# Router logits made tile by tile, three experts ranked and read first, latent weights read behind the last store

## The chip, the cores and the metric

The kernel is one program on one core of a Trainium2 chip. Its engines are TensorE (PE in the profile), VectorE (DVE), ScalarE (ACT), GpSimd (POOL) and SyncE (SP), which here only issues transfers; 16 DMA engines move data between the chip's memory (HBM) and the on-chip SBUF. Each engine works through its own list of instructions in order and waits on semaphores for the others. The metric is the device time of one execution in microseconds.

## The reference, cut to what matters

1024 tokens of width 1024 pass through a first block (windowed attention, a gated recurrence and a delta-rule recurrence, side by side). Its output, with 16 meta tokens ahead of it (L = 1040 rows), passes through two layers. Each layer ends in a mixture of experts:

```python
p_g = softmax(xf @ wr_g + br_g)            # 4 groups, the best one is taken
logit_e = xf @ wr_e + br_e                 # 32 experts, 8 in a group
top_v, top_i = top_k(sel, 2)               # two experts in the chosen group
y = (silu(xb @ w_gate[e]) * (xb @ w_up[e])) @ w_down[e]
out[token] += y * gate
```

Layer 0 mixes by pooled windows ahead of its experts. After its experts the shared latent is computed: `c = rmsnorm(h) @ w_dkv`, then keys and values by `w_uk` and `w_uv`, and queries by `w_dq` and `w_uq`. Layer 1 mixes by attention over that latent, then an output projection, then its experts; the end is an RMS norm. All is float32.

## The kernel before

Rows are held as tiles of 128: eight of them (NT = 8), and in layer 0 a ninth, first in order, for the 16 meta rows (NS = 9). One python function per engine and stage writes that engine's list; `pe_moe`, `act_moe`, `dve_moe`, `pool_moe` and `sp_moe` (from L2933) put a layer together: routing turns, the table, the experts, overflow blocks.

**Routing turns.** `turns(n, depth)` interleaves the steps of the tiles: in turn t each step d works on tile t - d, the latest step first. In layer 0 the steps are row scaling for the pool (d = 0), pooled windows (d = 1), the group map and the sum into h (d = 2: VectorE L1805, GpSimd L1834, ScalarE's square sum L1538), root and scaled rows (d = 3: L1612, L1609, L1926), transposes of the rows (d = 4: TensorE L1878, ScalarE copies L1907), logits (d = 5: TensorE in `mm`, L218). In layer 1 they are the output projection (d = 0: 32 records of TensorE a tile), root and rows, transposes and logits. `mm` and `transpose` write float32; one product in the code is two records in the trace. Before the change `routed` says at which tiles logits are made: the meta tile alone, tiles 0 to 3 at tile 3, tiles 4 to 6 at tile 6, tile 7 alone. The weights `wr` (128x36) are the stationary side and give logits transposed, 36 rows high; ScalarE copies them out (L1913), TensorE transposes them back (L1895), VectorE adds the bias (L1933). PSUM banks are given out in the order of the list that `plan_layer` builds; `rb.free(key)` is the wait for the bank's last user.

**Table.** VectorE alone, save for two TensorE steps: it picks experts, counts tokens per expert, sorts the 32 experts by count (`y.key` = count times 32 plus `y.backward`, L2011; eight ranks at a time, each counted by the semaphore `sorted`) and computes which token goes to which row of which block. TensorE turns that into the list `idx` by one-hot products (16 or 18 of 128x128 by 41 columns).

**Experts.** 25 blocks of 128 rows. The 18 experts with most tokens (N_BIG) have a block each, the other 14 share seven blocks in pairs of 64 rows (`PAIR_AT` says at which places). An expert with more tokens than its rows needs an overflow block, worked serially behind the 25 (`sp_over` and its like), as many as the data ask for. `sp_experts` loads weights in order of rank through four buffers, 2 MB of gate and up (L2121) and 1 MB of down (L2126) for each; `weights_of` waits for the sort and reads the expert's number from `by_count`. Loads 0 to 2 go out at the start, load 3 when gathers 0 and 1 have landed, later ones when TensorE has used the buffer. GpSimd gathers each block's rows from `xn_dram` (L2264) once `idx` is there; TensorE transposes them (L2139), multiplies gate and up, transposes the hidden rows (L2161), multiplies down; SyncE stores each block's result (L2279).

**Latent stage.** In the last blocks of layer 0 `sp_latent_ahead` also loads `wc`, the rope table, `w_uv`, `w_uq` (behind block 22) and `w_uk` (behind block 23). When the last stores have landed, GpSimd gathers the two expert rows of each token (L2378), VectorE sums them into h (L2372), ScalarE squares and takes the root (L1538, L1612), VectorE scales the rows (L2612), TensorE transposes (L2527) and multiplies. `dve_latent` first scales `w_uq` (three instructions, L2592) and `w_uv` (two, L2594); `w_uk` is scaled ahead of the fourth tile's sum.

Of the kernel before, what the change touches and what calls it, by code (L numbers as in the profile page):

```python
# [57 lines left out]
LOADED = [(_rank, _i) for _i in range(NM) for _rank in RANKS[_i]]  # L58
SLOTS = NBLK * P
# [127 lines left out]
def build(nc, io):  # L187
    ctx = ExitStack()
    with ctx:
# [27 lines left out]
        def mm(e, out, lhsT, rhs, start, stop):  # L217
            return e.matmul(out, lhsT, rhs, start=start, stop=stop, skip_group_check=True)  # L218
# [1398 lines left out]
        def routed(y, p):  # L1617

            s = y.slots[p]
            if s == NT:  # L1620
                return NT, NT
            return {3: (0, 3), NT - 2: (4, NT - 2), NT - 1: (NT - 1, NT - 1)}.get(s)

        layers, ring_before, table_before = [], [o1], [bk_]

        def plan_layer(layer):
# [17 lines left out]
            y.ci, y.full = take(P), take(NE)  # L1644
# [6 lines left out]
            for d, p in turns(y.ns, y.depth):  # L1651
# [6 lines left out]
                if d == y.norm_at + 2 and routed(y, p):  # L1658
                    order += [(("lgT", p), "S"), (("lg", p), "V")]
# [189 lines left out]
        def dve_ids(e, y):  # L1849
# [8 lines left out]
            e.tensor_scalar(y.backward, y.io32, -1.0, float(NE), ALU.mult, ALU.add).then_inc(*y.ids.up())  # L1858
# [11 lines left out]
        def pe_route(e, y, d, p):  # L1870
# [9 lines left out]
            elif d == y.norm_at + 2 and routed(y, p):  # L1880
                s0, s1 = routed(y, p)
                n = s1 + 1 - s0
                cols = slice(P * s0, P * (s1 + 1))
                key = ("lgT", p)
# [3 lines left out]
                for k in range(KD):  # L1888
                    m = mm(e, y.rb.bank[key][0:NR, 0:P * n], y.wr[:, k, :], y.xgT[:, k, cols], k == 0, k == KD - 1)
                m.then_inc(*y.rb.fill(key))  # L1890
                e.wait_ge(*y.rb.empty(key))
                key = ("lg", p)
                wait_all(e, y.rb.free(key))
                for j in range(n):
                    m = e.transpose(y.rb.bank[key][:, NR * j:NR * j + NR], y.lgT[0:NR, P * (s0 + j):P * (s0 + j + 1)], ident[0:NR, 0:NR])  # L1895
                m.then_inc(*y.rb.fill(key))

        def act_route(e, y, d, p):
# [10 lines left out]
            elif d == y.norm_at + 2 and routed(y, p):  # L1909
                s0, s1 = routed(y, p)  # L1910
                key = ("lgT", p)
                e.wait_ge(*y.rb.full(key))
                e.activation(y.lgT[0:NR, P * s0:P * (s1 + 1)], y.rb.bank[key][0:NR, 0:P * (s1 + 1 - s0)], ACT.Copy,  # L1913
                             bias=0.0).then_inc(*y.rb.drain(key, "S"))

        def dve_route(e, y, d, p):
# [11 lines left out]
            elif d == y.norm_at + 2 and routed(y, p):  # L1928
# [1233 lines left out]
```

## Time and profile before

| | us |
|---|---|
| median of 3 runs | 2188.95 |
| lowest, highest | 2187.75, 2190.74 |
| the profiled execution | 2186.3 |
| its span | 2184.6 |

In the profiled execution TensorE is busy for 1960.5 us (90%), VectorE for 807.5, ScalarE for 533.0, GpSimd for 188.3. By stage, in microseconds from the start of the span: the first block to about 679; routing turns of layer 0 to 787; table to 825; experts to 1131; latent stage from there and attention to 1649; routing turns of layer 1 to 1793; table to 1828; experts to 2136; the last sums and norm to the end. Times in rows are from the start of the span. A timeline row is start, duration, engine, line, operation, output from input, the shape of one instruction and how many were merged; the bracket is the idle time before and what ended it.

### The profile page before, as it was taken

The numbers are of one execution on the slowest core, as the hardware profiler recorded it, in microseconds if no ns is written. First come the engines' busy times: TensorE is split into PE (matmuls) and PEld (weight loads), VectorE is DVE, ScalarE is ACT, GpSimd is POOL, SyncE is SP. The second block draws the span as 40 slices with busy tenths as digits, with TensorE's granted clock in tenths as the row PEclk, the third lists the DMA queues.
The fourth block names the chain that finished last, engine by engine and source line by source line (L and its number), as shares of the span: only waits on it lengthen the run. The fifth ranks groups of instructions, "written<-read, shape, count | busy, mean of one in ns | idle before, by whom it ended". The sixth has DMA issues, their size and how long they took to land. (4 is left out here: it accounts for less than half of the span.)

```text
span 2184.6 us, 27881 instructions
## 1 busy us (share of the span) xinstructions
PE 1960.5 (90%) x10832; PEld 1121.7 (51%) x10832; DVE 807.5 (37%) x1849; ACT 533.0 (24%) x1295; POOL 188.3 (9%) x283
## 2 busy tenths in 40 slices
PE   8999999889997948999967999999999975999990
PEld 4545554578444824444424657677674433444440
DVE  1115557767254452111114534444451124111115
ACT  1003334433011311111123433333331110111112
POOL 0000002001262201000002000000000000000003
PEclk9999999899998968999988999999999986999995
DMA  3500100020011128999983000000010007999986
GB/s 135 224 32 1 39 20 4 1 80 4 34 65 44 57 115 342 410 424 424 426 361 122 22 1 1 1 1 1 1 78 23 39 29 314 364 426 423 425 356 261
DMA packets 51389, 334.67 MB, mean 153 GB/s; under 512 B 6832, under 2 KB 7152, under 8 KB 33200
## 3 DMA queue, kind: packets, MB, share of 16 engines
q1 hardware_dynamic: 39376, 289.63, 32.6%
q0 software_dynamic: 11872, 43.13, 5.3%
q8 instruction: 92, 1.51, 0.3%
q14 instruction: 49, 0.40, 0.1%
HBM read 285.48 MB, written 47.25 MB: 152 GB/s over the span
## 5 line engine op out<-in xcount | busy, mean ns | idle before, releaser
L218 PE MATMUL psum<-arena 64*64 64x64 f32 (+9 forms) x9424 | 1813.4, 385 | 120.5 <-DVE arena L2070 26.8
L218 PEld LDWEIGHTS psum<-arena 128*128 128x128 f32 (+3 forms) x9424 | 966.7, 165 | 908.2 <-issue 794.6
L2178 DVE TENSOR_TENSOR arena<-psum,arena 128x256 f32<-128x256 f32 x50 | 21.2, 425 | 430.4 <-ACT arena L2228 421.5
L1538 ACT ACTIVATE arena<-arena 128x1024 f32<-128x1024 f32 x43 | 45.4, 1056 | 249.9 <-DVE arena L2921 101.6
L2264 POOL DMA_INDIRECT arena<-xn_rows,arena x50 | 47.1, 943 | 685.6 <-PE psum L2139 453.7
L2228 ACT ACTIVATE arena<-psum 128x256 f32<-128x256 f32 x50 | 19.2, 385 | 328.2 <-PE psum L218 328.2
L2834 ACT ACTIVATE arena<-psum,arena 128x1024 f32<-128x1024 f32 (+8 forms) x72 | 50.2, 699 | 188.6 <-DVE arena L2870 188.6
L1239 ACT ACTIVATE arena<-psum 128x256 f32<-128x256 f32 (+3 forms) x128 | 43.9, 356 | 101.4 <-PE psum L218 90.3
L2139 PE MATMUL psum<-arena 128*128 128x128 f32 x400 | 53.7, 279 | 15.6 <-DMA arena<-xn_rows,arena 15.6
L2221 ACT ACTIVATE arena<-psum 128x512 f32<-128x512 f32 x50 | 29.9, 597 | 148.0 <-PE psum L218 148.0
L2863 DVE TENSOR_TENSOR psum<-psum,arena 128x128 f32<-128x128 f32 (+2 forms) x72 | 20.4, 283 | 103.5 <-PE psum L218 103.2
L2139 PEld LDWEIGHTS psum<-arena 128*128 128x128 f32 x400 | 46.6, 144 | 16.9 <-DMA arena<-xn_rows,arena 15.9
L2251 DVE COPY arena<-psum 128x512 f32<-128x512 f32 x50 | 34.6, 692 | 53.5 <-PE psum L218 53.5
L2209 ACT ACTIVATE arena<-psum 128x512 f32<-128x512 f32 x50 | 29.9, 598 | 98.8 <-PE psum L2139 98.8
L2372 DVE SCALAR_TENSOR_TENSOR arena<-arena 128x1024 f32<-128x1024 f32 (+1 forms) x34 | 43.6, 1281 | 25.5 <-DMA arena<-expert_rows,arena 24.0
L2865 DVE TENSOR_REDUCE arena<-psum 128x1 f32<-128x1024 f32 (+8 forms) x72 | 50.8, 706 | 2.5
L2378 POOL DMA_INDIRECT arena<-expert_rows,arena x34 | 34.6, 1019 | 192.6 <-issue 135.9
L2886 DVE COPY arena<-psum 128x512 f32<-128x512 f32 (+3 forms) x48 | 22.8, 490 | 76.0 <-PE psum L2789 75.9
L2789 PE MATMUL psum<-arena 128*128 128x128 f32 x352 | 48.9, 273 | 0.0
L381 ACT ACTIVATE arena<-psum 128x512 f32<-128x512 f32 (+1 forms) x26 | 15.5, 597 | 127.3 <-PE psum L218 127.3
L395 DVE TENSOR_TENSOR arena<-psum,arena 128x512 f32<-128x512 f32 x16 | 10.9, 689 | 84.2 <-ACT arena L376 84.0
L639 DVE TENSOR_TENSOR arena<-psum,arena 128x512 f32<-128x512 f32 (+1 forms) x32 | 18.8, 651 | 62.4 <-PE psum L218 62.4
(303 smaller groups left out, 1298.1 us busy)
## 6 DMA issues: line engine op xcount, KB each, us to landing
arena<-in_w_exp SPq DMA_DIRECT2D x64, 2048.0 KB, 18.7
arena<-in_w_exp SPq DMA_DIRECT2D x64, 1024.0 KB, 20.6
expert_rows<-arena SPq DMA_DIRECT2D x66, 512.0 KB, 15.8
arena<-in_x SPq DMA_DIRECT2D x16, 512.0 KB, 4.3
xn_rows<-arena SPq DMA_DIRECT2D x16, 512.0 KB, 2.6
arena<-in_w_out SPq DMA_DIRECT2D x8, 512.0 KB, 7.8
arena<-in_w_o SPq DMA_DIRECT2D x1, 4096.0 KB, 12.1
out<-arena SPq DMA_DIRECT2D x8, 512.0 KB, 4.2
```

Source lines behind the costliest of these rows:

```text
L218: return e.matmul(out, lhsT, rhs, start=start, stop=stop, skip_group_check=True)
L1239: e.activation(dst, src, ACT.Copy, bias=0.0).then_inc(*ring.drain((i, name), "S"))
L1538: return e.activation(junk, h[:, s, :], ACT.Square, accum_out=sq_sum[:, s:s + 1])
L2139: m = e.transpose(four(ring.bank[key])[:, k, :], xe[:, P * (4 * hf + k):P * (4 * hf + k + 1)], ident)
L2209: e.activation(y.xt[b % 2][:, 4:8, :], four(y.ex.bank[key]), ACT.Copy, bias=0.0).then_inc(*y.ex.drain(key, "S"))
L2251: e.tensor_copy(y.y[b % 3][:, half_cols(0)], y.ex.bank[key]).then_inc(*y.ex.drain(key, "V"))
L2264: e.indirect_dma_start(out=xe, out_offset=None, in_=xn_dram[:, :], in_offset=bass.IndirectOffsetOnAxis(idx.bitcast(I32)[:, block:block + 1 ...
L2372: e.scalar_tensor_tensor(out=h[0:n, s, :], in0=c[j][0:n, :], scalar=gates[0:n, s, j:j + 1], in1=h[0:n, s, :], op0=ALU.mult, op1=ALU.add).t ...
L2378: e.indirect_dma_start(out=c[j][0:n, :], out_offset=None, in_=y_dram[:, :], in_offset=bass.IndirectOffsetOnAxis(dest.bitcast(I32)[0:n, s, ...
L2789: m = e.transpose(four(sd.bank[key])[:, j, :], pb[:, kp:kp + P], ident)
L2834: e.activation(pb[0:n, p0:p1], part_bank(key).bank[key][0:n, 0:p1 - p0], ACT.Exp, bias=mx[0:n, 0:1], scale=SCALE, accum_out=rsu[0:n, u:u + ...
L2865: e.tensor_reduce(mx[0:n, u:u + 1], bk[0:n, 0:p1 - p0], AX.X, ALU.max).then_inc(*V.up())
```

## The change

- Logits are made for each tile by itself: the tile's rows are the stationary side (128x128), `wr` moves (36 columns), and the result comes out with tokens on partitions. The copy by ScalarE, the small transposes and the function `routed` go.
- Experts 0, 1 and 2 get ranks 0, 1 and 2 whatever their counts: `y.backward` is raised by 65536 times 3, 2 and 1 for them, by two more VectorE instructions. `weights_of` returns their fixed addresses without a wait, so loads 0 to 2 go out when the routing turns are over.
- `w_uq`, `w_uv` and `w_uk` are loaded behind the last expert's store; VectorE's scaling of `w_uq` and `w_uv` moves ahead of the third tile's sum.
- ScalarE takes one root of a constant behind the overflow blocks of each layer, which loads the root's table there.

```diff
@@ -1614,13 +1617,6 @@
-        def routed(y, p):
-
-            s = y.slots[p]
-            if s == NT:
-                return NT, NT
-            return {3: (0, 3), NT - 2: (4, NT - 2), NT - 1: (NT - 1, NT - 1)}.get(s)
@@ -1655,8 +1651,8 @@
-                if d == y.norm_at + 2 and routed(y, p):
-                    order += [(("lgT", p), "S"), (("lg", p), "V")]
+                if d == y.norm_at + 2:
+                    order.append((("lg", p), "V"))
@@ -1855,7 +1851,11 @@
-            e.tensor_scalar(y.backward, y.io32, -1.0, float(NE), ALU.mult, ALU.add).then_inc(*y.ids.up())
+            e.tensor_scalar(y.backward, y.io32, -1.0, float(NE), ALU.mult, ALU.add).then_inc(*V.up())
+
+            e.tensor_scalar(y.lead, y.io32, float(N_FIRST), 0.0, ALU.subtract, ALU.min).then_inc(*V.up())
+            e.wait_ge(*V.last())
+            e.scalar_tensor_tensor(out=y.backward, in0=y.lead, scalar=-float(LEAD), in1=y.backward, op0=ALU.mult, op1=ALU.add).then_inc(*y.ids.up())
@@ -1877,22 +1877,13 @@
-            elif d == y.norm_at + 2 and routed(y, p):
-                s0, s1 = routed(y, p)
-                n = s1 + 1 - s0
-                cols = slice(P * s0, P * (s1 + 1))
-                key = ("lgT", p)
+            elif d == y.norm_at + 2:
+                key = ("lg", p)
                 e.wait_ge(*y.m_router)
                 e.wait_ge(*y.rb.empty(("xt", p, 1)))
                 wait_all(e, y.rb.free(key))
                 for k in range(KD):
-                    m = mm(e, y.rb.bank[key][0:NR, 0:P * n], y.wr[:, k, :], y.xgT[:, k, cols], k == 0, k == KD - 1)
-                m.then_inc(*y.rb.fill(key))
-                e.wait_ge(*y.rb.empty(key))
-                key = ("lg", p)
-                wait_all(e, y.rb.free(key))
-                for j in range(n):
-                    m = e.transpose(y.rb.bank[key][:, NR * j:NR * j + NR], y.lgT[0:NR, P * (s0 + j):P * (s0 + j + 1)], ident[0:NR, 0:NR])
+                    m = mm(e, y.rb.bank[key][:, 0:NR], y.xgT[:, k, P * s:P * (s + 1)], y.wr[:, k, :], k == 0, k == KD - 1)
                 m.then_inc(*y.rb.fill(key))
...
@@ -2111,6 +2093,8 @@
             rank = LOADED[n][0]
+            if rank < N_FIRST:
+                return io["w_exp"][y.n * NE + rank]
             e.wait_ge(*y.sorted.at(rank // 8 + 1))
@@ -2395,14 +2379,13 @@
-                assert top_uq <= base_b2 + 2 * WG and {n % 4 for later in range(b + 1, NM) for n in y.of[later]} == {2, 3}
-                e.wait_ge(*y.ex.full(("gu", b)))
-                e.dma_start(w_uv, io["w_uv"]).then_inc(d_lu.sem, 16)
-                e.dma_start(w_uq, io["w_uq"]).then_inc(d_lu.sem, 16)
-            if b == NM - 2:
-                assert top_uq + 2 * MH * NOPE <= base_b2 + 3 * WG and {n % 4 for n in y.of[NM - 1]} == {3}
-                e.wait_ge(*y.ex.full(("gu", b)))
-                e.dma_start(w_uk, io["w_uk"]).then_inc(d_uk.sem, 16)
+
+        def sp_latent_behind(e):
+
+            assert top_uq + 2 * MH * NOPE <= base_b2 + 3 * WG
+            e.dma_start(w_uq, io["w_uq"]).then_inc(d_lu.sem, 16)
+            e.dma_start(w_uv, io["w_uv"]).then_inc(d_lu.sem, 16)
+            e.dma_start(w_uk, io["w_uk"]).then_inc(d_uk.sem, 16)
@@ -2434,6 +2417,8 @@
             sp_store(e, y, NM - 1)
+            if y.n == 0:
+                sp_latent_behind(e)
@@ -2587,12 +2572,13 @@
         def dve_latent(e):
-            e.wait_ge(*m_lu)
-            for k in range(3):
-                e.tensor_scalar(w_uq[:, k, :], w_uq[:, k, :], col("q_norm", k), None, ALU.mult).then_inc(*(lat_w if k == 2 else V).up())
-            for k in range(2):
-                e.tensor_scalar(w_uv[:, k, :], w_uv[:, k, :], col("kv_lat", k), None, ALU.mult).then_inc(*lat_w.up())
             for d, s in turns(NS, LAT):
+                if (d, s) == (0, 2):
+                    e.wait_ge(*m_lu)
+                    for k in range(3):
+                        e.tensor_scalar(w_uq[:, k, :], w_uq[:, k, :], col("q_norm", k), None, ALU.mult).then_inc(*(lat_w if k == 2 else V).up())
+                    for k in range(2):
+                        e.tensor_scalar(w_uv[:, k, :], w_uv[:, k, :], col("kv_lat", k), None, ALU.mult).then_inc(*lat_w.up())
@@ -2954,6 +2940,8 @@
             act_experts(e, y)
             act_over(e, y)
 
+            e.activation(scr[:, 0:1], one_col, ACT.Sqrt).then_inc(*S.up())
```

The bias is then added per tile (`y.lg[:, s, :]` from the bank's 36 columns and `y.br`), and ScalarE's branch for logits is removed. `N_FIRST` is 3 and `LEAD` is 65536.

## Rows read from the trace of the kernel before

**Rows 1.** The page: memory traffic in GB/s, 40 equal slices of the span.

```profile
GB/s 135 224 32 1 39 20 4 1 80 4 34 65 44 57 115 342 410 424 424 426 361 122 22 1 1 1 1 1 1 78 23 39 29 314 364 426 423 425 356 261
```

**Rows 2.** Timeline of layer 0's routing turns, TensorE and VectorE.

```profile
734.12 7.17 PE L218 MATMUL psum<-arena 128*128 128x256 f32 x48 [0.34 <-issue]
...
742.56 14.16 PE L218 MATMUL psum<-arena 128*128 128x256 f32 x64 [0.34 <-issue]
...
757.76 1.09 PE L1878 MATMUL psum<-arena 128*128 128x128 f32 x8
...
775.07 7.02 PE L218 MATMUL psum<-arena 128*36 128x384 f32 x16 [3.45 <-issue]
...
775.38 1.28 DVE L1926 SCALAR_TENSOR_TENSOR arena<-arena 128x1024 f32<-128x1024 f32 x1
...
782.96 1.09 PE L1878 MATMUL psum<-arena 128*128 128x128 f32 x8
...
787.39 0.20 DVE L1933 TENSOR_TENSOR arena<-psum,arena 128x36 f32<-128x36 f32 x1 [4.06 <-PE psum L1895]
```

**Rows 3.** Timeline of layer 1's routing turns, TensorE and VectorE.

```profile
1735.41 20.89 PE L218 MATMUL psum<-arena 128*128 128x512 f32 x48
...
1758.27 13.90 PE L218 MATMUL psum<-arena 128*128 128x512 f32 x32
...
1776.81 1.97 PE L1878 MATMUL psum<-arena 128*128 128x128 f32 x8 [3.76 <-DVE arena L1926]
...
1779.51 8.29 PE L218 MATMUL psum<-arena 128*36 128x384 f32 x16 [0.73 <-issue]
...
1793.11 0.20 DVE L1933 TENSOR_TENSOR arena<-psum,arena 128x36 f32<-128x36 f32 x1 [4.05 <-PE psum L1895]
```

**Rows 4.** Timeline of the first weight load, gather and transposes, layers 0 and 1.

```profile
805.34 0.36 SPq L2121 DMA_DIRECT2D arena<-in_w_exp  x1
...
825.26 1.18 POOL L2264 DMA_INDIRECT arena<-xn_rows,arena  x1 [52.45 <-DVE arena L2088]
...
831.57 1.97 PE L2139 MATMUL psum<-arena 128*128 128x128 f32 x8 [6.84 <-DMA arena<-xn_rows,arena]
...
1828.43 0.98 POOL L2264 DMA_INDIRECT arena<-xn_rows,arena  x1 [178.23 <-DVE arena L2088]
...
1836.66 1.97 PE L2139 MATMUL psum<-arena 128*128 128x128 f32 x8 [8.74 <-DMA arena<-xn_rows,arena]
```

**Rows 5.** Timeline from the last stores of layer 0 into the latent stage.

```profile
1125.99 5.01 SPq L2279 DMA_DIRECT2D expert_rows<-arena  x2
...
1133.57 2.88 DVE L2592 TENSOR_SCALAR arena<-arena 128x1536 f32<-128x1536 f32 x3 [4.58 <-DMA arena<-in_w_uq]
...
1142.31 0.94 POOL L2378 DMA_INDIRECT arena<-expert_rows,arena  x1 [66.59 <-issue]
...
1146.83 1.28 DVE L2372 SCALAR_TENSOR_TENSOR arena<-arena 128x1024 f32<-128x1024 f32 x1 [9.06 <-DMA arena<-expert_rows,arena]
...
1151.51 1.28 ACT L1612 ACT_TABLE_LOAD   x1
...
1171.51 0.69 DVE L2618 COPY arena<-psum 128x512 f32<-128x512 f32 x1 [9.30 <-PE psum L2527]
```

**Rows 6.** Timeline of layer 0's table, the one-hot products.

```profile
816.83 7.90 PE L218 MATMUL psum<-arena 128*128 128x41 f32 x36 [13.64 <-DVE arena L2070]
```

**Rows 7.** Busy time and granted clock, 1770 to 1790 us; clock after the engines.

```profile
1770.00:1790.00 20.00, 14.71 (x49) 6.67 (x47) 3.86 (x6) 4.79 (x11) 0.00 (x0) 0.74 0.13 53
```

**Rows 8.** Chain of waits, layer 1's last store and first gather: start, us, what.

```profile
2136.05 4.50 DMA expert_rows<-arena
...
2142.05 0.94 POOL arena L2378
```

**Rows 9.** Timeline of the last stage, first sum.

```profile
2146.46 1.29 DVE L2372 SCALAR_TENSOR_TENSOR arena<-arena 128x1024 f32<-128x1024 f32 x1 [12.11 <-DMA arena<-expert_rows,arena]
```

**Rows 10.** The page, costliest groups: the gathers of expert rows.

```profile
L2264 POOL DMA_INDIRECT arena<-xn_rows,arena x50 | 47.1, 943 | 685.6 <-PE psum L2139 453.7
```

## What the change will do to the time

> **What bounds the kernel now.** The page's 40 slices of 54.6 us come first [rows 1]: memory traffic stands at 340 to 426 GB/s only in the expert streams, layer 0's in slices 16 to 21 and layer 1's in 35 to 39; elsewhere it is low and cannot be the bound. The change touches five places around these streams, so the timeline of each was read: the routing turns of both layers [rows 2, 3], the table and the first rows of the experts [rows 4], and the passage from the last expert of layer 0 to the latent stage [rows 5]. The reader should look for what released the first TensorE instruction of each stage. It is a chain, not a queue of work: logits, then table, then a gather, then TensorE; last store, then a gather, then sum, root, transpose, TensorE. Whatever leaves those chains comes off the end in full, because what follows is ordered behind them. Inside the streams TensorE runs back to back and nothing of the change lies there.
>
> **Logits, layer 0.** Today the first tile's logits are made alone, tiles 0 to 3 in one batch of 16 records of 512 columns, tiles 4 to 6 in one of 384, and tile 7 alone; each batch is followed by a ScalarE copy and small transposes. The new form has 16 records per tile with 128x128 weights and 36 columns. No row shows 36. Nearest are 128x128 weights with 41 columns: 7.90 us for 36, 0.22 us each, at the low clock [rows 6]. At the high clock, the ordinary turn has 48 records in 7.17 us [rows 2]; 16 of them have 256 columns (0.22 us each, as the batch's 0.43 us for 512 tells), which leaves 0.11 us each for the 32 narrow ones. So a tile costs 1.8 us high and 3.5 us low; I take 1.8 in the turns, which have no pause, and lean to 3.5 at the tail, where TensorE pauses. In a turn it waits 0.34 us [rows 2], so 1.8 us adds 1.45 to each of five turns, +7.3 us. Removed there: 14.16 - 7.17 = 7.0 us of the batch, 1.0 us of copy and transposes behind it (742.56 + 14.16 to 757.76) and 0.8 us of the same for the first tile. Net -1.5. The end is where it pays: from 775.07 to 782.96 the last tile's transposes stand behind the batch of three, 7.9 us, though their rows are ready at 776.7. With one tile in the batch's place this is 1.8 to 3.5 us. From 782.96 to the last logits at 787.39 is 4.4 us; afterwards it is transposes 1.1 to 2.0, copy 0.7, logits 1.8 to 3.5, 3.7 to 6.3 in all. The last logits come 8.1 us earlier at the high clock, 3.9 at the low. I take **-5.5**.
>
> **Logits, layer 1.** The turns hold 32 records of 512 columns and are all TensorE [rows 3]: four tiles add 7.2 us and the batch takes away 20.89 less 13.9, 7.0 us, and 1.0 us behind it: -0.8. The tail: before, transposes at 1776.81, the batch of three in 8.29 us from 1779.51, last logits at 1793.11. Afterwards two of the three are made while TensorE waits for tile 6's rows anyway (it waits 3.76 us there), and the third lies between transposes. Following the same chain (ScalarE copy 1.1, root 0.3, reciprocal 0.2, row scaling 1.3, transposes 1.1, copy 0.7, logits) gives 1784.1 at the high clock and 1788.4 at the low. The granted clock there is 0.74 of full speed [rows 7], a mix of the two levels, and the same transposes take 1.97 us there and 1.09 in layer 0 [rows 2]. I take **-6.0**, between -4.7 and -9.0.
>
> **Experts 0 to 2 read early.** Their three loads go out at 805.34 behind the sort; now they go behind the last logits, some 18 us sooner. This does not start the stream sooner by 18 us: TensorE starts when the first gather lands, and that is issued after the table (825.26). The gain is only that the gather runs on idle DMA engines. It takes 6.3 us in layer 0 and 8.2 in layer 1 while the loads run [rows 4]; the first gather of the last stage, with nothing beside it, takes 4.4 [rows 8, 9]. So **-1.8** and **-3.7** (bounds 1.0 to 2.3 and 2.5 to 4.3). The loads of later experts wait for buffers that TensorE frees and so shift with it. What hides the early loads is the table, 38 us from the last logits to the gather against 22 us for 9.4 MB at 424 GB/s [rows 1]. Behind these issues on SyncE stand only the fourth expert's loads, which wait for gathers 0 and 1 anyway. The forced ranks add two short VectorE operations with a wait ahead of layer 0's first rows: **+0.3**; in layer 1 they lie in an idle stretch.
>
> **Latent weights behind the last store.** They stand in the queue ahead of the last stores today. The last store goes out at 1131.0 (the second of the pair in [rows 5]) and the first gather of the sums starts at 1142.31, 11.3 us later. In layer 1, with nothing beside it, the store lands 4.50 us after 2136.05 and the gather starts at 2142.05, 6.0 us [rows 8]. Without the 4.4 MB the gather should start near 1137. But the same 4.4 MB, 10.3 us of all engines, now run from 1133 to about 1144, under the gathers. A gather that is issued with about this much still to come took 8.2 us (layer 1, [rows 4]), not the 4.5 us seen here [rows 5]: it lands at 1145.3 to 1146.7 where it landed at 1146.8. The weights are then through, so the second should follow more closely. I take 1.7 us for both, between 0 and 3.7. The DMA page of the Trainium skill, "DMA: Bandwidth & Descriptors", section "Queues, rings and completion order", has each engine take turns between queues a packet at a time. By an equal share a gather would lose only its own 1.2 us of transfer, and this part would be worth some 2 us more; the trace of gathers beside weight loads says 3.8 us lost, and I go by that.
>
> The scaling of these weights on VectorE (2.88 us for three rows, so about 4.2 for all five) today hides in its wait for the store. It moves ahead of the third sum, where VectorE next waits 9.30 us for TensorE [rows 5]; 4.2 of that is free. Should the weights land after 1160 this cover is gone, and 1 us late costs 1 us. The gathers of later tiles wait for that sum, but have 12 us.
>
> **Root's table.** Its load of 1.28 us stands between square sum and root [rows 5], and behind it wait row scaling, the second tile's sum and, through ScalarE, the copy that lets TensorE start on the latent products: -1.3, with the gather part's 1.7 **-3.0** (bounds 0 and -5). In the last stage the load ends before VectorE is done with the second sum: nothing. The Trainium skill ("ScalarE: Activation LUTs", "What ACT_TABLE_LOAD costs") adds 1.38 us of draining to a load; no row here shows it, the root starts 20 ns after the load. With it the sum would be 1.4 us better.
>
> **Sum.** -5.5 - 6.0 - 1.8 - 3.7 + 0.3 - 3.0 = **-19.7 us**. The profiled execution took 2186.3 us (span 2184.6 and 1.7 around it), which gives 2166.6; the median of the runs is 2.65 above it, so 2188.95 - 19.7 = **2169.2**. All best ends give -28.5 (2160.5), all worst -11.6 (2177.4).
>
> **Rivals.** *The streams take the starts back.* DMA is full in them, and if loads, not TensorE, set their end, an earlier first gather changes nothing, and with the sums' gathers equally late only the logits and root's table are left: -11.5 - 1.3 + 0.3 = -12.5, 2176.5. For: 424 GB/s throughout, within 2 of the highest of the page [rows 1]. Against: TensorE has no pause in 200 us of them, and the loads are released by it. *The narrow records are dear*: 0.22 us in the turns too, because 128 columns of weights are loaded for 36 moved. Nine turns at +1.7 are +15.3, at the low ends of both tails: -3.9 - 4.7 + 15.3 - 5.2 - 3.0 = -1.5, 2187.5. Against: the 32 narrow ones of layer 0's turns. *Slower, by an overflow block*: ranking three fixed experts first pushes others out of the 18 full blocks of 128 rows; one of those with more than 64 tokens needs a serial block behind all others. Its price, from rows: weights about 10 us, gate and up 7, evictions and transposes 2.5, down 3.7, store and its landing 5, issue 2, about 30 us. A single one decides: 2169.2 + 30 = 2199. Against: 50 gathers, none extra, before [rows 10], and the reference's own router on its inputs gives 14 and 12 experts above 64 tokens, so with experts 0 to 2 added 15 and 15 places are needed of 18. It also needs other inputs. *The change doesn't do what it says*: if the loads still waited for the sort (they don't in the diff), the 5.5 us are missing: 2174.7, inside the range.
>
> **Chances.** The sum 0.72, streams take back 0.13, dear records 0.08, overflow 0.03, something worse that I don't see 0.04. The range of the sum, widened to the first rival and towards the second: **2160 to 2182**. What a measurement here can tell from no change is about 0.2%, 4.4 us. Faster 0.87, same 0.08, slower 0.05.
>
> **What would show it.** The last logits of layer 0 near 782 and the first weight loads at once behind them; first gather to TensorE 4.5 us in both layers; narrow groups of 16 in 1.8 us in the turns. First gather of the sums 6 us behind the last store but 8 us to land; no table load between square sum and root; VectorE's five scalings inside its wait for TensorE. Wrong if a turn of layer 0 is much above 9.9 us, if the last of the stream does not shift with its first, or if VectorE waits for the latent weights.

## The result and the profile after

| | us |
|---|---|
| before, median of 4 runs (lowest to highest) | 2189.84 (2187.75 to 2192.07) |
| after, median of 4 runs (lowest to highest) | 2171.03 (2164.63 to 2174.86) |
| ratio after to before, 95% interval | 0.9919 (0.9897 to 0.9940) |
| the profiled execution of after, its span | 2170.03, 2168.3 |

The change makes the kernel 18.8 us faster (2189.84 - 2171.03); the interval of the ratio is 13 to 23 us. The forecast was 19.7 us less, 2169.2.

The page of after has the traffic where [rows 1] had it, but for slices 15 (204 for 115) and 33 (81 for 29), into which the early loads of layers 0 and 1 now fall ahead of the streams, and 16 and 34, which have less (245 for 342, 278 for 314); and it has the same 50 gathers of expert rows as [rows 10], so no overflow block:

```profile
GB/s 136 213 34 11 39 20 4 1 81 4 2 98 44 49 204 245 404 423 425 424 368 158 23 1 1 1 1 1 1 78 23 29 81 278 379 426 423 425 354 263
...
L2248 POOL DMA_INDIRECT arena<-xn_rows,arena x50 | 47.3, 945 | 672.4 <-PE psum L2123 447.9
```

The timeline of TensorE in the routing turns of layer 0, after, answers [rows 2]. An ordinary turn first, then the tail:

```profile
728.89 1.07 PE L1878 MATMUL psum<-arena 128*128 128x128 f32 x8
729.80 8.90 PE L221 MATMUL psum<-arena 128*128 128x256 f32 x64
738.53 1.07 PE L1878 MATMUL psum<-arena 128*128 128x128 f32 x8
```

```profile
773.52 1.07 PE L1878 MATMUL psum<-arena 128*128 128x128 f32 x8
776.34 3.60 PE L221 MATMUL psum<-arena 128*128 128x36 f32 x16 [1.75 <-issue]
779.74 1.95 PE L1878 MATMUL psum<-arena 128*128 128x128 f32 x8
782.42 3.60 PE L221 MATMUL psum<-arena 128*128 128x36 f32 x16 [0.73 <-issue]
```

A turn takes 9.64 us (728.89 to 738.53), and its 64 records 8.90 where 48 took 7.17: 1.73 us for the 16 narrow ones, 0.11 us each. In the tail the same 16 take 3.60 us. The last of them releases VectorE, and SyncE's first weight load follows at once (timeline of both, after):

```profile
786.06 0.19 DVE L1916 TENSOR_TENSOR arena<-psum,arena 128x36 f32<-128x36 f32 x1 [5.89 <-PE psum L221]
...
786.32 0.33 SPq L2105 DMA_DIRECT2D arena<-in_w_exp  x1
```

The tail of layer 1 (TensorE, after) answers [rows 3]; its last logits are added at 1781.55:

```profile
1767.43 1.95 PE L221 MATMUL psum<-arena 128*128 128x36 f32 x16 [0.78 <-issue]
1769.21 1.88 PE L1878 MATMUL psum<-arena 128*128 128x128 f32 x8
1771.82 3.60 PE L221 MATMUL psum<-arena 128*128 128x36 f32 x16 [0.73 <-issue]
1775.23 1.95 PE L1878 MATMUL psum<-arena 128*128 128x128 f32 x8
1777.91 3.60 PE L221 MATMUL psum<-arena 128*128 128x36 f32 x16 [0.73 <-issue]
```

First gather and first transposes of both layers, after, answer [rows 4]. From the gather to TensorE it is 4.65 us in layer 0 and 4.31 in layer 1 (before 6.31 and 8.23):

```profile
823.89 1.18 POOL L2248 DMA_INDIRECT arena<-xn_rows,arena  x1 [49.81 <-DVE arena L2070]
...
828.54 1.97 PE L2123 MATMUL psum<-arena 128*128 128x128 f32 x8 [5.18 <-DMA arena<-xn_rows,arena]
...
1816.86 0.98 POOL L2248 DMA_INDIRECT arena<-xn_rows,arena  x1 [173.49 <-DVE arena L2070]
...
1821.17 1.97 PE L2123 MATMUL psum<-arena 128*128 128x128 f32 x8 [4.83 <-DMA arena<-xn_rows,arena]
```

The passage into the latent stage, after, answers [rows 5]:

```profile
1127.69 0.32 SPq L2263 DMA_DIRECT2D expert_rows<-arena  x1
...
1128.06 0.43 SPq L2386 DMA_DIRECT2D arena<-in_w_uq  x1
...
1133.72 0.94 POOL L2362 DMA_INDIRECT arena<-expert_rows,arena  x1 [60.79 <-issue]
...
1135.28 1.28 ACT L2943 ACT_TABLE_LOAD   x1
...
1142.28 1.28 DVE L2356 SCALAR_TENSOR_TENSOR arena<-arena 128x1024 f32<-128x1024 f32 x1 [16.29 <-DMA arena<-expert_rows,arena]
1145.99 1.28 DVE L2356 SCALAR_TENSOR_TENSOR arena<-arena 128x1024 f32<-128x1024 f32 x1 [2.42 <-DMA arena<-expert_rows,arena]
...
1155.24 2.86 DVE L2579 TENSOR_SCALAR arena<-arena 128x1536 f32<-128x1536 f32 x3
...
1166.37 0.69 DVE L2604 COPY arena<-psum 128x512 f32<-128x512 f32 x1 [4.37 <-PE psum L2512]
```

The first and the second sum are the additions of the first tile's two expert rows; each waits for a gather of its own. The gather starts 5.71 us behind the end of the last store's issue, where it was 11.31 (1131.00 to 1142.31). But the first sum comes 8.56 us behind it instead of 4.52, and the second 3.71 behind the first. Before, that was 2.20, as the timeline of before shows:

```profile
1146.83 1.28 DVE L2372 SCALAR_TENSOR_TENSOR arena<-arena 128x1024 f32<-128x1024 f32 x1 [9.06 <-DMA arena<-expert_rows,arena]
1149.03 1.28 DVE L2372 SCALAR_TENSOR_TENSOR arena<-arena 128x1024 f32<-128x1024 f32 x1 [0.91 <-DMA arena<-expert_rows,arena]
```

The intervals below are read from the timelines of one profiled execution each; "route start" is GpSimd's first instruction of the routing turns, "to last logits" ends where VectorE adds the bias to them, "to last store" runs from the experts' first transposes to the start of the last store's issue, "last store to first gather" from the end of that issue, "c0" is the first latent product, "c2" the third tile's transposes in the latent stage. The c0 to c2 of busy all is left out, because unused products stand ahead of c0 there.

| interval, us | before | before again | after | after again | logits only | early only | latent only | latent late | busy tail | busy all | best |
|---|---|---|---|---|---|---|---|---|---|---|---|
| start to route start, layer 0 | 679.3 | 682.0 | 681.9 | 686.5 | 678.9 | 681.0 | 684.0 | 679.7 | 686.8 | 683.3 | 684.8 |
| to last logits, layer 0 | 108.1 | 107.8 | 104.1 | 104.1 | 100.9 | 108.8 | 107.6 | 104.2 | 100.0 | 100.4 | 99.5 |
| first gather to TensorE, layer 0 | 6.3 | 6.2 | 4.7 | 5.0 | 6.3 | 5.3 | 6.5 | 4.8 | 4.6 | 4.8 | 5.7 |
| to last store, layer 0 | 299.1 | 299.9 | 299.2 | 299.9 | 298.7 | 299.1 | 299.6 | 300.4 | 300.1 | 296.9 | 295.8 |
| last store to first gather of the sums | 11.3 | 10.2 | 5.7 | 5.1 | 11.1 | 10.1 | 4.5 | 6.1 | 6.1 | 5.5 | 5.7 |
| first gather of the sums to first sum | 4.5 | 4.5 | 8.6 | 8.7 | 4.5 | 4.3 | 9.1 | 4.2 | 8.7 | 8.5 | 4.1 |
| first sum to second | 2.2 | 1.7 | 3.7 | 3.5 | 2.1 | 2.0 | 3.8 | 2.2 | 2.6 | 3.1 | 2.5 |
| second sum to transposes | 5.1 | 5.1 | 3.8 | 3.8 | 5.1 | 5.1 | 5.1 | 3.8 | 3.8 | 3.8 | 3.8 |
| c0 to c2 | 26.6 | 23.6 | 24.1 | 23.9 | 26.7 | 23.5 | 26.5 | 26.2 | 23.7 | | 26.4 |
| route start to last logits, layer 1 | 143.8 | 142.3 | 139.1 | 139.3 | 139.8 | 142.2 | 143.8 | 140.1 | 134.2 | 134.2 | 134.2 |
| first gather to TensorE, layer 1 | 8.2 | 8.4 | 4.3 | 4.9 | 7.4 | 4.4 | 8.4 | 5.1 | 4.9 | 5.0 | 5.0 |
| to last store, layer 1 | 299.4 | 300.2 | 298.8 | 300.0 | 300.1 | 298.6 | 299.0 | 298.5 | 299.7 | 295.3 | 295.2 |

### The profile page after: what moved, and what is told of

It reads as the page before. It is cut to its first block and busy times, and to the rows that moved or that the text cites. A ratio compares the mean times of both kernels' runs of the same rounds, so it can differ in the third digit from the quotient of the medians.

```text
span 2168.3 us, 28117 instructions
## 1 busy us (share of the span) xinstructions
PE 1961.4 (90%) x10975; PEld 1146.7 (53%) x10975; DVE 809.5 (37%) x1863; ACT 531.4 (25%) x1290; POOL 189.3 (9%) x283
## 5 line engine op out<-in xcount | busy, mean ns | idle before, releaser
L221 PE MATMUL psum<-arena 128*128 128x512 f32 (+12 forms) x9584 | 1817.1, 384 | 117.5 <-DVE arena L2052 26.7
L221 PEld LDWEIGHTS psum<-arena 128*128 128x128 f32 (+3 forms) x9584 | 994.5, 169 | 887.3 <-issue 774.8
L2907 DVE TENSOR_TENSOR arena<-arena,psum 128x512 f32<-128x512 f32 x16 | 11.0, 688 | 84.3 <-PE psum L221 84.3
```

## The experiments

The theory is that of the sum: logits, early loads and latent stage each take their term off a chain. The rivals are that the streams take the earlier starts back, that narrow records are dear, and, once the result was seen, that the clock takes a part of the logits' gain. The first three kernels carry one part of the change each; the early root was not run alone.

| kernel | median us (runs) | before beside it | ratio, 95% |
|---|---|---|---|
| logits only | 2174.94 (2172.70 to 2179.48) | 2189.58 | 0.9942 (0.9922 to 0.9961) |
| early only | 2178.38 (2175.48 to 2182.95) | 2189.58 | 0.9957 (0.9939 to 0.9974) |
| latent only | 2190.40 (2185.95 to 2194.56) | 2189.58 | 1.0008 (0.9995 to 1.0021) |
| after again | 2173.92 (2168.73 to 2175.22) | 2189.58 | 0.9922 (0.9902 to 0.9943) |
| latent weights behind the gathers | 2170.65 (2170.30 to 2180.51) | 2190.64 | 0.9910 (0.9884 to 0.9935) |
| busy tail | 2164.16 (2161.22 to 2166.91) | 2190.64 | 0.9876 (0.9850 to 0.9903) |
| busy all | 2158.68 (2149.51 to 2164.35) | 2190.64 | 0.9854 (0.9813 to 0.9894) |
| latent late | 2164.88 (2163.48 to 2166.06) | 2189.75 | 0.9890 (0.9872 to 0.9908) |
| best | 2153.15 (2152.22 to 2153.57) | 2189.75 | 0.9838 (0.9824 to 0.9853) |

### Logits tile by tile, alone

The kernel before with only this part (`mm` in the new form, the copy, the small transposes and `routed` gone):

```diff
-                    m = mm(e, y.rb.bank[key][0:NR, 0:P * n], y.wr[:, k, :], y.xgT[:, k, cols], k == 0, k == KD - 1)
...
+                    m = mm(e, y.rb.bank[key][:, 0:NR], y.xgT[:, k, P * s:P * (s + 1)], y.wr[:, k, :], k == 0, k == KD - 1)
```

> The kernel before with the logits tile by tile and nothing else. My theory, corrected by the trace of the changed kernel: the two tails each gain, but at the low level of TensorE's clock, 3.6 us for 16 narrow records, so last logits come about 4 us earlier in layer 0 (from the start of its routing turns) and 4.7 in layer 1, and the median falls by 8 to 9 us. A turn of layer 0 takes 9.6 us instead of 8.4, paid back by the missing batch. Rival, that the profiled gain is an accident of the clock: the two intervals from the start of the routing turns to the last logits change by less than 2 us each and the median by under 4.

Measured: 14.6 us faster than before (2189.58 - 2174.94; 8.5 to 17.1 by the interval), where 8 to 9 was expected. Layer 1 gives 4.0 in the profile, layer 0 gives 7.2, 11.2 together; the rest of the 14.6 isn't explained. That dear narrow records cost the gain is ruled out: they cost 0.11 us in the turns. Why layer 0 gives more than in after (4.0) stands in the tail of this kernel's timeline (TensorE): the first narrow group there still takes 1.95 us, and only what follows is slow.

```profile
768.95 1.07 PE L1871 MATMUL psum<-arena 128*128 128x128 f32 x8
771.76 1.95 PE L218 MATMUL psum<-arena 128*128 128x36 f32 x16 [1.74 <-issue]
773.54 1.90 PE L1871 MATMUL psum<-arena 128*128 128x128 f32 x8
776.18 3.60 PE L218 MATMUL psum<-arena 128*128 128x36 f32 x16 [0.73 <-issue]
```

That is 1.7 us of the 3.2, and 0.3 is the forced ranks, which this kernel lacks; the rest lies in the first turns, which also run in part at the lower level (clock 0.84 over their first 40 us, 0.81 in after). The same code gains more or less by where in it the clock falls.

### Experts 0 to 2 read early, alone

```diff
+            if rank < N_FIRST:
+                return io["w_exp"][y.n * NE + rank]
```

with the raised `y.backward`.

> The kernel before with experts 0 to 2 ranked first and read early, nothing else. My theory: only the first gather's flight shortens, from 6.3 to about 4.6 us in layer 0 and from 8.2 to about 4.3 in layer 1, minus 5.6 us in all, kept to the end of both streams; two VectorE operations cost 0.3 us. Median lower by 5 us. Rival, that the stream is bound by its transfers and takes the start back: the interval from the first rows on TensorE to the last store grows by as much as the flight shrinks, and the median moves by under 1 us. A second rival, that the stream starts 19 us sooner and gains far more: median lower by over 10 us.

Measured: 11.2 us faster (5.7 to 13.4 by the interval). In the profile the gathers' flights are 1.0 and 3.8 us shorter, and the experts take 299.1 and 298.6 us, no longer than in before: the streams don't take the start back. The profile's intervals give 4.8 us of gathers and 0.8 of the second stream, 5.6 in all, the low edge of the interval. Intervals that no line of this part touches give more: c0 to c2 3.2, layer 1's turns 1.6, last store to first gather of the sums 1.2. All three are as short in a second execution of before, so they are not shown to be the change's. The second rival on record has the right size, over 10 us, but not the mechanism: the first gather still starts 37.9 us behind layer 0's last logits, so the stream starts no 19 us sooner. So the forecast of 5.2 holds for the mechanism; a part of the 11.2 of the median isn't explained.

### Latent weights behind the last store, alone

```diff
+            e.dma_start(w_uq, io["w_uq"]).then_inc(d_lu.sem, 16)
+            e.dma_start(w_uv, io["w_uv"]).then_inc(d_lu.sem, 16)
+            e.dma_start(w_uk, io["w_uk"]).then_inc(d_uk.sem, 16)
```

behind `sp_store(e, y, NM - 1)`, the scaling ahead of the third sum, and no early root.

> The kernel before with the latent weights behind the last store (and their scaling moved), nothing else, root's table still loaded late. My theory: the first gather of the sums starts 6 us earlier after the last store, but lands 8.5 us after its start where it took 4.5, and the second 3.7 us behind the first, so the second sum starts about 0.4 us earlier than before and TensorE's first latent transposes as well; median lower by 0 to 1 us. Rival, that the earlier start carries through: 3 us or more at TensorE's transposes.

Measured: 0.8 us slower over ten runs, between 1.1 faster and 4.6 slower. Its timeline of VectorE and GpSimd has the two sums 9.13 and 12.91 us behind the gather, where before has 4.52 and 6.72:

```profile
1140.40 0.94 POOL L2378 DMA_INDIRECT arena<-expert_rows,arena  x1 [60.52 <-issue]
...
1149.53 1.28 DVE L2372 SCALAR_TENSOR_TENSOR arena<-arena 128x1024 f32<-128x1024 f32 x1 [15.62 <-DMA arena<-expert_rows,arena]
1153.31 1.28 DVE L2372 SCALAR_TENSOR_TENSOR arena<-arena 128x1024 f32<-128x1024 f32 x1 [2.49 <-DMA arena<-expert_rows,arena]
```

What the earlier gather gains, the 4.4 MB beside it take back in full.

### After and before once more

Both without an edit, to see how much an interval of a profile moves by itself.

> The changed kernel once more, to see what differs from one execution to the next. If the 2.7 us that it was late ahead of the routing turns, where the code is the same, and the 2.5 us that it gained between the second and third latent product are the clock's, then another profile shows either one changed while the intervals of the changed steps agree within 0.5 us. If they belong to the change, both stand again.

> The kernel before once more, one look. If the start of the routing turns and the step from the first to the third latent product move with the clock from execution to execution, this profile differs from the first of before by microseconds there, while the gather's flights (6.3 and 8.2 us), store to gather (11.6) and gather to first sum (4.5) stand within 0.5 us. If they are constants of the kernel, all agree within 0.5 us.

Measured: after again 2173.92, ratio 0.9922, where the first time gave 0.9919; one execution of before took 2184.49. In the table most steps of the change repeat within 0.6 us. The exceptions are layer 1's turns of before, 143.8 and 142.3, so their gain is between 2.9 and 4.7; last store to first gather of the sums, 11.3 and 10.2 in before, so that gain is between 4.5 and 6.2; and the streams, which move by up to 1.2. Two intervals that no edit touches move more: start to route start is between 678.9 and 687.2 us in twelve profiles with the same code up to there, and c0 to c2 is 26.6 or 23.6 in two profiles of before. The windows of the two profiles of before show what it is in c0 to c2 (before, then before again; stretch, its length, busy time of PE, PEld, DVE, ACT and POOL, granted clock, DMA share, GB/s): the same stretch has a clock of 0.82 and 0.90.

```profile
1157.00:1187.00 30.00, 26.40 (x86) 16.72 (x86) 11.59 (x23) 9.14 (x25) 5.61 (x6) 0.82 0.33 105
```

```profile
1157.00:1187.00 30.00, 24.52 (x91) 15.96 (x90) 13.26 (x25) 10.40 (x28) 5.70 (x6) 0.90 0.33 110
```

So the end of a single profile tells a gain only to some us, and an interval around a step to one or two.

### Latent weights behind the gathers

From after: the call of `sp_latent_behind` leaves `sp_experts` and stands behind the overflow blocks, with a wait for the second pair of gathers.

```diff
-            if y.n == 0:
-                sp_latent_behind(e)
...
+            if y.n == 0:
+                wait_all(e, m_cl[1])
+                sp_latent_behind(e)
```

> The changed kernel with the latent weights read only when the gathers of the first two tiles have landed. My theory, that the weights slow these gathers: first sum 4.5 us after the first gather instead of 8.6, second sum 2.1 behind it instead of 3.6, so TensorE's first latent transposes come 5.5 us earlier than in the changed kernel, and the weights, landing some 22 us after the first gather, still meet VectorE in its wait for TensorE; median 4 to 5.5 us below the changed kernel. Rival, that gathers are slow there for another reason (their own queue, the store just before): first sum stays 8.6 us after the gather, and the median rises by up to 5 us because the weights come late. A second rival: the gathers are fast but VectorE waits for the weights ahead of the third sum and gives it back.

Measured: 2170.65, which can't be told from after. The profile is of its slowest execution, 2180.5, where the other four took 2170.3 to 2173.9. The sums come 4.35 and 6.45 us behind the gather again, so it was the 4.4 MB that delayed them. But now VectorE waits for the weights (its timeline in this kernel; the loads go out from 1152.15):

```profile
1157.31 0.89 DVE L2596 TENSOR_SCALAR arena<-arena 128x1024 f32<-128x1024 f32 x1
1165.92 2.88 DVE L2577 TENSOR_SCALAR arena<-arena 128x1536 f32<-128x1536 f32 x3 [7.73 <-DMA arena<-in_w_uv]
1168.72 1.41 DVE L2579 TENSOR_SCALAR arena<-arena 128x1024 f32<-128x1024 f32 x2
1170.04 2.67 DVE L2356 SCALAR_TENSOR_TENSOR arena<-arena 128x1024 f32<-128x1024 f32 x2
```

c0 to c2 takes 31.2 us in it, 7.1 more than in after. Of this 6.0 is TensorE's wait ahead of the second tile's products (7.91 us for 1.93), the rest its clock. So the wait that is taken away at the gather comes back at the scaling, in front of the third tile's sums: the second rival on record.

### Latent late: the scaling moved as well

The same kernel, with the scalings two tiles later:

```diff
-                if (d, s) == (0, 2):
+                if (d, s) == (0, 4):
...
-                if (d, s) == (0, 3):
+                if (d, s) == (0, 5):
```

> The changed kernel with the latent weights read when the first two tiles' gathers have landed, and their scaling moved two tiles later, ahead of the fifth and sixth tiles' sums, where VectorE waits for TensorE anyway. My theory, from the run before: first sum 4.4 us after the gather, second 2.1 behind, no wait of VectorE for the weights, so the steps from first gather to the third tile's latent transposes take about 38.5 us where the changed kernel took 44.3 and the run with the early scaling 45; median 5 us below the changed kernel, about 2166. Rival, that the delay is only moved on: the fifth tile's sum comes late, TensorE waits there, and from the third tile's transposes to the start of layer 1's routing turns it takes over 3 us more than the 464.2 of all other runs.

Measured: 2164.88; the ratio is 0.9890 against 0.9919 and 0.9922 of after, some 6.6 us, though the intervals overlap (0.9872 to 0.9908, 0.9897 to 0.9940). In its timeline of VectorE both sums are early, and no wait for the weights is left:

```profile
1137.52 1.28 DVE L2356 SCALAR_TENSOR_TENSOR arena<-arena 128x1024 f32<-128x1024 f32 x1 [12.27 <-DMA arena<-expert_rows,arena]
1139.75 1.29 DVE L2356 SCALAR_TENSOR_TENSOR arena<-arena 128x1024 f32<-128x1024 f32 x1 [0.95 <-DMA arena<-expert_rows,arena]
...
1154.72 1.28 DVE L2356 SCALAR_TENSOR_TENSOR arena<-arena 128x1024 f32<-128x1024 f32 x1 [4.45 <-DMA arena<-expert_rows,arena]
1160.48 0.69 DVE L2602 COPY arena<-psum 128x512 f32<-128x512 f32 x1 [4.48 <-PE psum L2510]
```

From the first gather to c0 this wins 5.9 us. The later gathers now run beside the weights (the wait at 1154.72 is for one of them), but TensorE waits no longer for it: 1.93 us ahead of the second tile's products, as in before and after. From c0 to layer 1's route start it takes 490.2 us instead of 488.4; all of this is in c0 to c2 (26.2 for 24.1), which differs by 3 us between the two profiles of before, and from c2 on it is 464.0 for 464.2. So nothing shows that any of the 5.9 is given back.

### Busy tail: the clock held up

From after: TensorE multiplies the identity with ones, 512 columns wide, into the bank that the logits are to fill, while it waits for ScalarE's copy. The products are used by nobody.

```diff
+        def keep_busy(e, bank, n):
+            for _ in range(n):
+                mm(e, four(bank), ident, bc_mid(ones, 4), True, True)
...
-                e.wait_ge(*y.rb.empty(("xt", p, 1)))
                 wait_all(e, y.rb.free(key))
+                if p >= y.ns - 3:
+                    keep_busy(e, y.rb.bank[key], 2 if y.n == 0 and p == y.ns - 2 else 1)
+                e.wait_ge(*y.rb.empty(("xt", p, 1)))
```

> The changed kernel with one or two wide products of constants, 512 columns, ahead of the logits of the last three tiles of either layer, in TensorE's pauses; results unused. My theory, that the narrow records cost 3.6 instead of 1.9 us at the tails because the clock is at its low level there: with the pauses filled the clock holds, the last logits come 3 us earlier in each layer and the median falls by up to 6 us. Rival, that 0.22 us is the narrow record's own price after a pause or that the clock falls anyway: the last logits come 1 to 4 us later by the added work.

Measured: 2164.16. The windows of the last turns of layer 0, columns as above (the clock is the third from the end), in before, after and busy tail:

```profile
774.00:790.00 16.00, 10.57 (x44) 5.01 (x44) 4.21 (x33) 4.27 (x8) 0.00 (x0) 0.86 0.08 33
```

```profile
774.00:790.00 16.00, 9.54 (x46) 8.82 (x44) 5.05 (x39) 5.01 (x9) 0.08 (x1) 0.56 0.25 86
```

```profile
774.00:790.00 16.00, 12.76 (x83) 10.24 (x81) 7.07 (x39) 4.90 (x9) 2.49 (x2) 1.00 0.29 101
```

After loses the high level in the tail (0.56, where 0.50 is the level of 1.2 GHz), which before mostly has (0.86). With the pauses filled it is 1.00, and last logits come 100.0 and 134.2 us behind route start, 4.1 and 4.9 less than in after. That shows that the clock, not the order of work, was what kept the gain small.

### Busy all: the same at the other pauses

The same products also in the table (12 behind the last logits, 12 ahead of the one-hot products), ahead of the first gather's transposes (5) and ahead of the latent stage (20, and 3 ahead of its first product).

> As the one before, with such products also in TensorE's waits of the table (12 and 12), of the first gather (5) and of the latent stage's first rows (20 and 3). My theory: the clock stays at its high level over these waits; the first expert block's products take 6.9 us instead of 9 to 10 in both layers, the first latent products fall from 11.6 to about 8 us for the first tile and likewise the second; with the tails 12 to 16 us below the changed kernel. Rival, that the clock falls all the same: the products run at the low level, last twice as long, and push the table's products and first rows back, 5 to 20 us slower than the changed kernel.

Measured: 2158.68. The experts take 296.9 and 295.3 us instead of 299.2 and 298.8, as the stream now begins at the high level (clock 1.00 over the first 20 us in both layers, 0.78 and 0.85 in after), and from last logits to first gather it is 36.6 and 34.1 us instead of 37.8 and 35.3. The latent stage gained nothing, against the expectation: the unused products end 3.60 us ahead of the first transposes, these still take 1.97 us, and from the first gather of the sums to c2 it takes 45.5 us (44.5 in after).

### Best: both together

Latent late and busy all, with 18 products instead of 20 and without the 3.

> The one before together with the unused wide products in TensorE's pauses: at the tails of the routing turns, in the table's waits, ahead of the first expert rows, and 18 ahead of the first latent rows, none between these and the latent products. My theory: the two savings add, since one shortens a chain and the other the work at its end: about 2152 to 2155, with the first expert block at the high level of the clock in both layers and the first latent products at 8 to 9 us instead of 11.6. Rival, that the clock's low stretches only move to other places: the low stretches of the profile sum to as much as in the changed kernel, 244 us, and the median is that of the run with the tails filled, 2164, or above.

Measured: 2153.15, 1.6% below before (0.9824 to 0.9853 of it) and 17.9 below the first median of after. The mean granted clock over the span is 0.970 (before 0.948, after 0.944). The rival, that the low stretches only move, falls. The timeline of TensorE at the first expert of layer 0, after and best: the first 16 products take 10.17 and 7.11 us.

```profile
831.29 10.17 PE L221 MATMUL psum<-arena 128*128 128x512 f32 x16 [0.78 <-ACT arena L2193]
```

```profile
828.98 7.11 PE L221 MATMUL psum<-arena 128*128 128x512 f32 x16 [0.78 <-ACT arena L2204]
```

In layer 0's table the unused products of best run into the landing of the first gather: the transposes follow them without a pause, 5.7 us behind the gather, where busy all has a pause of 0.63 and 4.8 us.

And the passage to the latent stage in best (TensorE), with the products of the same tile in latent late below it: the unused products end 0.51 us ahead of the transposes, so they delay nothing, and the transposes take 1.09 us where after has 1.97.

```profile
1139.45 1.09 PE L2524 MATMUL psum<-arena 128*128 128x128 f32 x8 [0.51 <-DVE arena L2610]
1143.74 12.38 PE L221 MATMUL psum<-arena 128*128 128x384 f32 x32 [3.20 <-issue]
```

```profile
1147.88 12.12 PE L221 MATMUL psum<-arena 128*128 128x384 f32 x32 [2.33 <-issue]
```

But a pause follows, and the first latent products take as long as without any unused ones, where 8 to 9 us was expected. From the first gather of the sums to c2 best takes 41.2 us and latent late 40.7. So the gain of the unused products is that of the tails, the tables and the experts' starts; at the latent stage no profile shows one.

## Why the prediction was right, step by step

The total was right, 2169.2 against 2171.0, but in part by luck: the terms that the profiles show sum to 16.2 us, not 19.7. The steps as the profiles of before and after have them, in us:

| step | forecast | bounds | measured |
|---|---|---|---|
| logits and forced ranks, layer 0 | -5.2 | -7.8 to -3.6 | -4.0 |
| logits, layer 1 | -6.0 | -9.0 to -4.7 | -4.7 |
| first gather, layer 0 | -1.8 | -2.3 to -1.0 | -1.7 |
| first gather, layer 1 | -3.7 | -4.3 to -2.5 | -3.9 |
| gathers of the sums | -1.7 | -3.7 to 0 | -0.1 |
| root's table | -1.3 | | -1.3 |
| the two streams | 0 | | +0.1, -0.6 |
| sum | -19.7 | | -16.2 |

The medians differ by 18.8 and, the second time, by 15.7; the profiled executions by 16.3 (2186.3 - 2170.03). The second profiles of both give +0.9 for the gathers of the sums (-5.1 + 4.2 + 1.8), -2.9 for layer 1's logits, and -11.9 for the sum. So the steps explain 12 to 16 us, and the rest is within what runs differ by: the intervals that no edit touches moved by +2.7 and -2.5 us between the two profiles.

- **Logits: mechanism right, size off.** The term that failed is where I stood between the bounds. I leaned to the low clock only for part of the tail, and both layers came out near the low-clock end: in layer 0 -3.9 + 0.3 = -3.6 forecast there and -4.0 measured, in layer 1 -4.7 and -4.7 (-3.2 against the second profile of before). Redone from its rows, the prediction's high-clock end for layer 0 is 8.3 us, not 8.1, and the ends of all terms are -28.4 and -11.8; neither moves the forecast. I read the clock of the tail of before, 0.74 [rows 7] and full speed in layer 0 [rows 2], and carried it over. But the batch of three tiles, which the change takes away, was also what kept TensorE busy there: busy tail puts other work in its place and gets the high-clock ends: -8.1 us in layer 0 (108.1 to 100.0; -7.8 forecast there, the ranks in it) and -9.6 in layer 1 (143.8 to 134.2; -9.0 there).
- **Narrow records.** 0.11 us each in the turns, a turn 9.64 us against 9.9 forecast. The forced ranks' 0.3 us is in the wait ahead of the first product of the routing turns, 10.25 us in after and 9.93 in logits only.
- **Early loads.** As forecast in both layers: loads right behind the last logits, gather to TensorE 4.7 and 4.3 us (5.0 and 4.9 the second time). The rival that the streams take the start back falls: the experts take what they took, 299.2 and 298.8 us for 299.1 and 299.4.
- **Gathers of the sums.** The gather starts 5.7 us behind the last store (6.0 forecast), and lands 8.6 behind its start (8.2 forecast). What failed is the sentence that the second would then follow more closely: it comes 3.7 us behind the first instead of 2.2. So all of the term is gone, -5.6 + 4.0 + 1.5 = -0.1. The two kernels that move the loads away from the gathers and add nothing else (4.35 and 4.17 us to the first sum, 2.1 and 2.2 to the second) show that it is the loads' doing. In the Trainium skill, "DMA: Bandwidth & Descriptors", section "Queues, rings and completion order", engines take turns between queues packet by packet. The estimate that the prediction drew from it, that an equal share costs a gather about its own 1.2 us, is not what the runs show: beside the 4.4 MB the first gather loses 4.0 to 4.6 us. How the engines divided their turns is left open.
- **Scaling.** Its five instructions ended inside VectorE's wait: the copy behind them still waits 4.37 us for TensorE, of 9.30 before [rows 5]. The cover I named is real, and its limit too: when the weights come later, VectorE waits 7.73 us.
- **Root's table.** 5.11 us from the second sum to the transposes became 3.83 or 3.84 in all seven kernels with the edit: the 1.28 of the load. The 1.38 us of draining that the Trainium skill ("ScalarE: Activation LUTs", "What ACT_TABLE_LOAD costs") adds to a load did not come off.
- **Overflow block.** None, 50 gathers as before.

Open: why the parts alone sum to -25.0 us (-14.6, -11.2, +0.8), without the root's 1.3, and the whole is 15.7 to 18.8. In the profiles 3.2 us of it is layer 0's tail in logits only, whose clock fell later, and 3.2 is c0 to c2 in early only; the intervals of the three medians are wide enough for the rest.

## What to carry to other kernels

Take a stage apart by the chain that releases its first product, and sum only what leaves that chain; check that the same bytes or the same idle time don't come back one wait further on, as the latent weights did. A wide batch on TensorE ahead of a serial tail may be what holds the clock: before shortening it, price the tail at the lower level, and then fill the pauses with unused products that end just before the real ones are due. Where another pause follows, as in the latent stage, look whether anything is gained. Loads that are needed later go behind the gathers whose rows are awaited, and their first use goes as late as the order allows: only both moves together brought the gain.

## What the hardware showed that I had not expected

- Unused products of 512 columns, filling TensorE's pauses, raise the mean granted clock from 0.944 to 0.972 and take 12 us off (2171.0 to 2158.7, busy all), although they do nothing.
- Of the gathers of 0.5 MB beside 4.4 MB of loads the first releases its sum 8.5 to 9.1 us after the issue instead of 4.1 to 4.5, and the second 2.6 to 3.8 behind that instead of 1.7 to 2.5: both are late, not only the first.
- The granted clock falls at different points in executions of the same code: c0 to c2 took 26.6 us in one profile of before and 23.6 in the other (clock 0.82 and 0.90 over the same 30 us), and route start came between 678.9 and 687.2 us. That goes with the clock too: over the first 678 us it is 0.99 in the two profiles with the earliest route start (678.9 and 679.3) and 0.97 in the two with the latest (686.8 and 687.2).
